# First unit of each layer: where the sum of three weight tiles is made

## The reference

```
layer A:  h = rms_norm(x);  u, v, z = split(h @ a_w_in)        # a_w_in: 2048 x 12288
          x = x + (gelu(u) * (causal_mix(rms_norm(gelu(v))) + b) * silu(z)) @ a_w_out
layer B:  h = rms_norm(x);  q, k, v, z, f = split(h @ b_w_in)  # b_w_in: 2048 x 8208
          x = x + (forgetting_attention(norm(q), norm(k), v, f) * silu(z)) @ b_w_out
```

## Time and profile before

| what | value |
|---|---|
| median of three runs | 2358.54 us (2357.53 to 2359.57) |
| the profiled execution: own time, span | 2359.33 us, 2357.4 us |
| mean granted TensorE clock | 0.996 |
| PE busy | 2277.1 us, 97% of the span |
| DVE busy | 1617.6 us, 69% |
| ACT busy | 1065.7 us, 45% |
| bytes moved by DMA | 477.49 MB, mean 203 GB/s |
| unit 0 | its first matmul of weights at 16.98 us |
| unit 12 | its third step begins on PE at 1388.73 us |

### The profile page before, as it was taken

The page is one execution under the profiler, slowest core; times in us unless marked ns, Lnnn a source line. Parts: engine busy times, 40 slices in busy tenths (PEclk is TensorE's granted clock), DMA queues, the critical chain, the costliest instruction groups (busy, mean ns, idle before and its releaser), DMA issues.

```text
span 2357.4 us, 26512 instructions
## 1 busy us (share of the span) xinstructions
PE 2277.1 (97%) x10413; PEld 1857.8 (79%) x10413; DVE 1617.6 (69%) x1676; ACT 1065.7 (45%) x1319; POOL 144.8 (6%) x197
## 2 busy tenths in 40 slices
PE   6999999999999999999999989999999999999999
PEld 5787788788788878878888867777777777778887
DVE  8778777877877777763222467875877777566665
ACT  5755545454544444552222534443454444344432
POOL 0011011000000000000000000110110100111000
PEclk9999999999999999999999999999999999999999
DMA  7678777776776777765444566695686687834333
GB/s 243 225 252 269 242 249 237 227 241 211 243 231 216 234 219 240 237 223 167 99 115 114 128 139 171 197 278 160 200 276 206 193 280 229 306 124 161 107 94 116
DMA packets 233084, 477.49 MB, mean 203 GB/s; under 512 B 19872, under 2 KB 26576, under 8 KB 231936
## 3 DMA queue, kind: packets, MB, share of 16 engines
q1 hardware_dynamic: 191056, 366.53, 51.6%
q0 software_dynamic: 18768, 67.28, 8.1%
q10 hardware_dynamic: 23136, 41.98, 4.8%
HBM read 393.90 MB, written 81.82 MB: 202 GB/s over the span
## 4 chain that ended last, share of the span: by engine, by line
PE 74%; DVE 11%; issue 6%; DMA 6%; ACT 2%; POOL 1%; SPq 0%; DVEq 0%; ACTq 0%; POOLq 0%
PE ps L1210 16%; PE ps L1212 15%; PE ps L1211 15%; PE ps L1368 5%; PE ps L1367 5%; PE ps L1369 5%; DVE u_lo L1657 4%; DMA t_rows<-t 3%; PE ps L1590 3%; PE ps L1592 2%; PE ps L1591 2%; ACT u_hi L725 2%; DVE raw L1642 2%; PE ps L1457 1%; PE ps L1513 1%
## 5 line engine op out<-in xcount | busy, mean ns | idle before, releaser
L725 ACT ACTIVATE u_hi<-raw 128x1536 fp32r<-128x1536 f32 (+1 forms) x320 | 544.7, 1702 | 800.4 <-PE ps L1212 767.7
L1657 DVE TENSOR_TENSOR u_lo<-raw,u_hi 128x1536 fp32r<-128x1536 f32 (+1 forms) x320 | 647.1, 2022 | 253.1 <-ACT u_hi L725 252.3
L1210 PE MATMUL ps<-u_hi,x1h 128*128 128x512 f32 x1280 | 511.1, 399 | 51.3 <-DVE u_lo L1657 45.5
L1211 PE MATMUL ps<-u_lo,x1h 128*128 128x512 f32 x1280 | 501.9, 392 | 0.0
L1212 PE MATMUL ps<-u_hi,x1l 128*128 128x512 f32 x1280 | 501.5, 392 | 0.0
L1210 PE MATMUL ps<-u_hi,x2h 128*128 128x512 f32 x960 | 380.2, 396 | 2.9 <-DVE u_lo L1657 2.3
L1212 PE MATMUL ps<-u_hi,x2l 128*128 128x512 f32 x960 | 374.6, 390 | 0.0
L1211 PE MATMUL ps<-u_lo,x2h 128*128 128x512 f32 x960 | 374.5, 390 | 0.0
L1210 PEld LDWEIGHTS ps<-u_hi,x1h 128*128 128x128 f32 x1280 | 242.1, 189 | 130.2 <-DVE u_lo L1657 67.5
L1212 PEld LDWEIGHTS ps<-u_hi,x1l 128*128 128x128 f32 x1280 | 242.1, 189 | 52.0
L1211 PEld LDWEIGHTS ps<-u_lo,x1h 128*128 128x128 f32 x1280 | 242.3, 189 | 47.9
(11 more groups left out here) (232 smaller groups left out, 2426.4 us busy)
## 6 DMA issues: line engine op xcount, KB each, us to landing
raw<-in_a_w_in_dram SPq DMA_DIRECT2D x280, 512.0 KB, 4.4
raw<-in_b_w_in_dram SPq DMA_DIRECT2D x184, 512.0 KB, 4.8
t_rows<-t ACTq DMA_DIRECT2D x160, 256.0 KB, 4.8
raw<-t_rows SPq DMA_DIRECT2D x160, 256.0 KB, 4.7
w_raw<-in_a_w_out_dram SPq DMA_DIRECT2D x128, 256.0 KB, 2.9
w_raw<-in_b_w_out_dram SPq DMA_DIRECT2D x64, 256.0 KB, 2.8
vz<-vz_rows POOLq DMA_DIRECT2D x16, 512.0 KB, 5.5
t<-yT_rows SPq DMA_DIRECT2D x28, 256.0 KB, 3.6
```

Of the source, the lines that this page charges most:

```text
L725: act.activation(u_hi[:, u_of(g), 0:n, :], raw_of(g)[:, 0:n, :], ACT.Copy).then_inc(hi1_ready, 1)
L1210: pe.matmul(dst[:, t, :], a, u_hi[:, s, pos, :], start=first, stop=False, skip_group_check=more)
L1211: pe.matmul(dst[:, t, :], a, u_lo[:, s, pos, :], start=False, stop=False, skip_group_check=more)
L1657: dve.tensor_tensor(u_lo[:, u_of(g), 0:n, :], raw_of(g)[:, 0:n, :], u_hi[:, u_of(g), 0:n, :].bitcast(F32), ALU.subtract).then_inc(lo1_read ...
```

## The change

In the first unit of each layer the sum of three tiles is no longer made in the first half, stored by ACT and read back. Instead the second half loads both k2 (512 KB) and k1 (512 KB, in place of the 256 KB of `t2_dram`), and DVE makes the sum there with two further adds over 128x512 in each step. The two further adds and the old one depend on each other, and each waits for the one ahead by a semaphore. The other units are as before, except that the store index `q` counts from the second unit on. Three pairs of semaphores are merged into one (`means_ready`), with the same waits.

```diff
+        def t2_of(u, k):
+            return (u - 1 - (u > UB)) * KP + k
...
                 else:
-                    q = u * KP + k
                     sp.dma_start(slot[:, 0:4:3, :], k2).then_inc(loaded, 16)
+                    if first(u):
+                        sp.dma_start(slot[:, 1:3, :], k1).then_inc(loaded, 16)
+                        return
+                    q = t2_of(u, k)
                     sp.wait_ge(t2_stored[q % 2], (q // 2 + 1) * 16)
                     sp.dma_start(slot[:, 2, :], t2_dram[k, :, :]).then_inc(loaded, 16)
...
                     high(0, 1, 0)
-                store_t2(0, k)
...
                     high(UB, 1, 0)
-                store_t2(UB, k)
...
                 else:
+                    if first(u):
+                        n = ((u == UB) * KP + k) * 2
+                        dve.tensor_tensor(m[:, 1, :], m[:, 0, :], m[:, 1, :], ALU.add).then_inc(t_part, 1)
+                        dve.wait_ge(t_part, n + 1)
+                        dve.tensor_tensor(m[:, 2, :], m[:, 1, :], m[:, 2, :], ALU.add).then_inc(t_part, 1)
+                        dve.wait_ge(t_part, n + 2)
                     dve.tensor_tensor(m[:, 1, :], m[:, 3, :], m[:, 2, :], ALU.add).then_inc(t_ready, 1)
...
             sums(0, 0, 0)
-            sum_t2(0, 0)
             x_sums(0)
             for k in range(KP):
                 if k + 1 < KP:
                     sums(0, 0, k + 1)
-                    sum_t2(0, k + 1)
                 else:
                     sums(0, 1, 0)
                 low(0, 0, k)
...
             for k in range(1, KP):
                 if k == 1:
-                    sum_t2(UB, 1)
                     low(UB, 0, 1)
                     sums(UB, 0, 2)
...
-                if k + 1 < KP:
-                    sum_t2(UB, k + 1)
```

More of the change, by code:

```diff
@@ L258, in build_trunk @@
         sq_ready = sem("sq_ready")
-        msa_ready = sem("msa_ready")
+        means_ready = sem("means_ready")
+        t_part = sem("t_part")
         rstda_ready = sem("rstda_ready")
@@ L267, in build_trunk @@
         v_stored = sem("v_stored")
-        vms_ready = sem("vms_ready")
         vrstd_ready = sem("vrstd_ready")
@@ L303, in build_trunk @@
         sqb_ready = sem("sqb_ready")
-        msx_ready = sem("msx_ready")
         rstd_ready = sem("rstd_ready")
@@ L470, in load_y @@
                 if k < 2:
-                    sp.wait_ge(t2_stored[k], VU * KP * 8 + ZU * KP * 8)
+                    sp.wait_ge(t2_stored[k], (NU - 1) * KP * 8)
                     if k == 0:
@@ L572, in power @@
                 return pool.tensor_tensor(dst, src, mhalf[:, 0:n], ALU.pow)
-            pool.wait_ge(msa_ready, 2)
+            pool.wait_ge(means_ready, 2)
             power(rstd_a[:, :], msx_a[:, 1, :], NT).then_inc(rstda_ready, 1)
@@ L601, in _ @@
                                    base=0, pattern=[[0, 4], [-1, P]], channel_multiplier=1).then_inc(ws_masked, 1)
-            pool.wait_ge(vms_ready, 2)
+            pool.wait_ge(means_ready, 4)
             power(vrstd[:, :], vms[:, 1, :], NT).then_inc(vrstd_ready, 1)
@@ L631, in _ @@
                 pool.dma_start(x2_dram[f, :, :, :], acc[f][:, :, :]).then_inc(x2_stored[f], 16)
-            pool.wait_ge(msx_ready, 2)
+            pool.wait_ge(means_ready, 6)
             power(rstd[:, :, 0], msx[:, 1, :], NT).then_inc(rstd_ready, 1)
@@ L1643, in sums @@
                 else:
+                    if first(u):
[4 more added lines that the diff above has]
+                        dve.wait_ge(t_part, n + 2)
                     dve.tensor_tensor(m[:, 1, :], m[:, 3, :], m[:, 2, :], ALU.add).then_inc(t_ready, 1)
             def sum_t2(u, k):
-                g, q = step_of(u, 0, k), u * KP + k
+                g, q = step_of(u, 0, k), t2_of(u, k)
                 dve.wait_ge(t_ready, g + 1)
@@ L1687, in x_stats_a @@
                 dve.wait_ge(sq_ready, KP * NT)
-                dve.tensor_reduce(msx_a[:, 0, :], ssx8[:, :, :], AX.X, ALU.add).then_inc(msa_ready, 1)
-                dve.wait_ge(msa_ready, 1)
+                dve.tensor_reduce(msx_a[:, 0, :], ssx8[:, :, :], AX.X, ALU.add).then_inc(means_ready, 1)
+                dve.wait_ge(means_ready, 1)
                 dve.tensor_scalar(msx_a[:, 1, :], msx_a[:, 0, :], 1.0 / D, EPS, ALU.mult, ALU.add)\
-                    .then_inc(msa_ready, 1)
+                    .then_inc(means_ready, 1)
                 dve.wait_ge(rstda_ready, 1)
@@ L1738, in v_stats @@
             def v_stats():
-                dve.tensor_reduce(vms[:, 0, :], vsq[:, :, :], AX.X, ALU.add).then_inc(vms_ready, 1)
-                dve.wait_ge(vms_ready, 1)
-                dve.tensor_scalar(vms[:, 1, :], vms[:, 0, :], 1.0 / AW, EPS, ALU.mult, ALU.add).then_inc(vms_ready, 1)
+                dve.tensor_reduce(vms[:, 0, :], vsq[:, :, :], AX.X, ALU.add).then_inc(means_ready, 1)
+                dve.wait_ge(means_ready, 3)
+                dve.tensor_scalar(vms[:, 1, :], vms[:, 0, :], 1.0 / AW, EPS, ALU.mult, ALU.add).then_inc(means_ready, 1)
             def z_silu(j, h):
@@ L1869, in x_means @@
                 dve.wait_ge(sqb_ready, NF * NT)
-                dve.tensor_reduce(msx[:, 0, :], ssx[:, :, :], AX.X, ALU.add).then_inc(msx_ready, 1)
-                dve.wait_ge(msx_ready, 1)
-                dve.tensor_scalar(msx[:, 1, :], msx[:, 0, :], 1.0 / D, EPS, ALU.mult, ALU.add).then_inc(msx_ready, 1)
+                dve.tensor_reduce(msx[:, 0, :], ssx[:, :, :], AX.X, ALU.add).then_inc(means_ready, 1)
+                dve.wait_ge(means_ready, 5)
+                dve.tensor_scalar(msx[:, 1, :], msx[:, 0, :], 1.0 / D, EPS, ALU.mult, ALU.add).then_inc(means_ready, 1)
                 dve.wait_ge(gains_loaded, 48)
@@ L1899, in _ @@
                             sums(UB, 0, 0)
-                            sum_t2(UB, 0)
                         elif k == 30:
```

## The result

The changed kernel takes 2366.17 us (median of 9 runs, 2362.43 to 2370.74); the kernel before, on the same chip, 2357.53 (9 runs, 2353.75 to 2360.86). The ratio is 1.0030, 95% interval 1.0020 to 1.0039: 8.6 us slower by the medians. The forecast was 2357.8 with a range to 2363.5, so the time lies above the range. The profiled execution took 2368.49 us (span 2366.6), 2.3 above its median.

A forecast was written before the change was run, and what follows sets the result against it. PE, busy 97% of the span, was taken as the bound, so only its waits could shrink. Unit 0's -1.1 and unit 12's +0.4 gave -0.7 us: 2357.8 against a median of 2358.54, range 2353.3 to 2363.5.

The forecast's parts named there:

- First halves: Units 0 and 12: sum and store gone; unit 0's step 6.49 to 5.77 us, unit 12's 3.25 us store wait gone.
- Unit 0, step 9: Second half of unit 0: step 9 starts on PE at 72.4 with a clock fall in step 7, 71.3 without.
- the gain of 1.1 us: Unit 0: what is left at step 9 of 3.9 us gained by step 6, given a clock fall in step 7.
- The six hidden steps 10 to 15: Second half of unit 0: cost nothing, DVE needing 5.12 us per step against PE's 5.44; cover left 0.3 us.
- The adds: Second halves of units 0 and 12: two further adds per step, 0.72 us each including the wait for the add before.
- the term c = 5.75: Unit 12: DMA time of 1 MB of weights, 5.75 us, more than PE's 5.44 per step; 0.4 us lost.
- Rival 2: Unit 12, steps 10 to 15: DMA queue becomes the bound; with 6.6 us per 1 MB +5.7, 2364.2 us; chance 0.15.
- the saturated row: DMA at 1398 to 1406 us, 93.7% busy: 5.96 us per 1 MB, weighed twice against the first bound.
- the unsaturated 5.3: DMA queue at 1422 to 1450 us, 60.5% busy: 5.3 us per 1 MB, the first of three bounds.
- the forecast's own price: Unit 12's second half: 7.5 us lost per us that a 1 MB load takes above 5.7.
- the landing of a lone load: Third bound on unit 12's loads: 768 KB landed 5.8 + 0.43 us after issue, giving 6.6 us per 1 MB.
- the 2.5 us of gain: Unit 12: gained if 1 MB takes 5.3 us, so that PE bounds from step 9 on.

The follow-up runs named there:

- T12: Not a run: the time from step 2 to step 15 of unit 12 on PE, 72.4 us before and 79.3 after.
- the nearer columns: Unit 12's two column blocks of b_w_in 4096 instead of 8192 bytes apart; ratio 0.9985 in the changed kernel, 0.9986 in the kernel before.
- one add: Changed kernel with only one of the three adds per step in unit 12's second half, all loads kept; 2359.58 us (1 run).
- columns (0, 0): Changed kernel with unit 12 reading blocks from columns 0 and 2048, again 8192 bytes apart; 2364.29 us (1 run).

## Why the prediction was wrong

**First halves: right in unit 0, not in unit 12.** In unit 0 a step of 5.77 was forecast and 5.75 measured, step 6 at 52.4 forecast and 51.67 measured. In unit 12 no wait for a store is left, but its first half got no shorter. PE's first matmul of step 8, before:

```profile
1422.60 0.50 PE L1210 MATMUL ps<-u_hi,x2h 128*128 128x512 f32 x1 [0.31 <-DVE u_lo L1657]
```

From step 2 to step 8 it is 33.9 us before (1388.73 to 1422.60) and 34.8 after (1391.36 to 1426.16), within the scatter of T12 but no gain. The waits for weights took the place of the wait for the store. With the nearer columns the same stretch is 30.0 us without the change and 28.3 with it, a gain at most there (1.7 us, also within the scatter).

**Unit 0, step 9: nearly right, and its end wrong.** `low` of step 7 was to end at 59.0 and did at 58.30. The clock fell in step 7 as expected, and `sum_57` waited 1.03 us for it. Step 9 came at 71.73, between the 71.3 without a fall and the 72.4 with one. The step that failed was to let the gain of 1.1 us stand from there on. PE still had 1.94 us of idle ahead of step 9, and the clock fell again at 73.2. Of the seven kernels with this unit 0, two fell less often there. From step 6 to unit 1 it is 67.6 us with two falls (after), 66.0 with one (one add) and 64.9 with none (columns (0, 0)). A fall costs 1.1 to 1.6 us here, and whether it comes is not fixed by the program. In unit 12 the clock stayed at 1.00 from 1398 to 1470 us through idles of 2.38, 2.23 and 2.36 us, longer than the 1.94 after which it fell in unit 0. The six hidden steps 10 to 15 were right: 0.22 us of cover, forecast 0.3.

**The adds.** Forecast 0.72 us each, measured 0.72 and 0.73. The Trainium skill ("VectorE: DVE Perf Modes", section on the DRAIN) says that semaphores between chained Vector instructions cost nothing extra. The trace differs again: the last add, for which `low` does not wait, is followed after 0.61 us (55.94 to 56.55).

**Unit 12: the term c = 5.75 was mis-sized, and it decides.** Rival 2 is what happened: the queue bounds steps 8 to 15. 1 MB occupies the queue for 5.96 us, as the saturated row said; I had weighed it down with the unsaturated 5.3. And a filled queue isn't full: three slots bound the loads, `low` must read a slot before the next load goes out, and each such turn leaves the queue short for a while (89.4%). The pace is 6.7 us. With the occupancy alone, c = 5.96, the forecast's sum gives 2.0 us lost; what it left out is the turn of a slot, since it let the loads of steps 12 to 15 "run back to back". By the forecast's own price, 7.5 x (6.7 - 5.75) = 7.1 us on top of 0.4 lost makes 7.5; measured 6.9. I had set the landing of a lone load aside as the slowest of 16 engines, which others would make up; it gave c = 6.6 and was right in size, which may be chance: the time to the last landing of one transfer alone and the pace of a slot-bound queue are different things, and nothing here shows that they go together.

What the rows could not show is why the loads are slow. I took 5.3 to 6.6 as the price of 1 MB of b_w_in; it is that of two pairs of columns. With the three others measured it is 3.2 to 3.6. Nor would a small c have brought the 2.5 us of gain: with the nearer columns T12 is 68.2 with the change and 68.4 without it, although DVE still waited 3.5 us for stores in the latter: with quick loads PE was idle for only 1.6 us behind step 2 there, so most of that wait lay beside PE's work.

The Trainium skill ("DMA: Bandwidth & Descriptors", section on bandwidth) has about 358 GB/s as the HBM limit for a core. With the DMA engines at 0.99 the window above shows 155 GB/s, so the rule gives no hint of this case; the window at 73 us in layer A shows 341 at 0.96.

**The sum.** Of two single executions, -0.2 for unit 0 and +6.9 for unit 12 make +6.7 of the 8.6 us between the medians. The other 2 us aren't assigned: they are less than the 2.2 us by which the interval of the ratio reaches to each side, and of the size of the scatter in T12 and in the time ahead of unit 12.

## What to carry to other kernels

Ask of each load what its own rows cost, not what its tensor costs: time per MB from the queue's share in a stretch where only this load runs, for each pair of columns. When a transfer replaces a wait and the queue is near the pace of PE, price it with the full round (slot free, issue, last landing), and take the slow end of the bounds when one us of it costs seven in the sum. A gain behind an idle of 2 us is not kept until the clock has stayed up past the next idle; the adds that nothing waits for can go behind the instruction that PE waits for, which left one long idle in unit 0 instead of two, but no measured time shows a gain from it.

## What the runs showed of the hardware

- Reads of two blocks of 2 KB per row, 128 rows each with a row pitch of 32,832 bytes: 1 MB occupied the queue for 5.96 us with columns from 1024 and 3072, 5.4 with 0 and 2048 (both 8192 bytes apart), but 3.3 at 4096 bytes apart and 3.2 at 10240. With 1536 and 3584, 8192 apart as well, it was 3.6. The rule behind it is open; no run moved the pair by less than a block.
- In the two first units TensorE's granted clock fell from 2.4 to 1.2 GHz for 3.4 or 6.8 us after idles of 1.9 to 3.1 us, and not after each of them. After the same idle of 2.3 us ahead of step 7 it fell in six kernels and not in a seventh, and in unit 12 of the changed kernel it stayed up after 2.2 to 2.4 us three times. So one profile does not say what a fall will cost the median.
